# Attention values summed by heads in column halves, with the row factors turned instead of the sums

## The reference, cut to what matters

```
p = masked_softmax(q @ k.T * scale, mask)                       # every branch
o_cmp, o_slc, o_win = p @ v                                      # NSA
o = g[:, :, 0] * o_cmp + g[:, :, 1] * o_slc + g[:, :, 2] * o_win # gates by token and head
y_a = o @ w_branch_nsa[layer]
y_b = dsa_mixer(...) @ w_branch_dsa[layer]
mixed = (gate[..., :D_MODEL] * y_a + gate[..., D_MODEL:] * y_b) @ w_out[layer]
```

## Time and profile before

| what | value |
| --- | --- |
| time, median of 3 runs | 1774.59 us (1774.58 to 1776.01) |
| time of the profiled execution | 1776.0 us |
| its span | 1774.0 us |
| mean granted TensorE clock | 0.979 |
| PE busy | 1672.5 us |
| DVE, ACT, POOL busy | 1250.1, 706.8, 614.2 us |
| attention steps | from 497.7 to about 914 us of the span |

### The profile page before, as it was taken

The page is one execution under the profiler, slowest core; times in us unless marked ns, Lnnn a source line. Parts: engine busy times, 40 slices in busy tenths (PEclk is TensorE's granted clock), DMA queues, the critical chain, the costliest instruction groups (busy, mean ns, idle before and its releaser), DMA issues.

```text
span 1774.0 us, 24401 instructions
## 1 busy us (share of the span) xinstructions
PE 1672.5 (94%) x8648; PEld 1356.2 (76%) x8648; DVE 1250.1 (70%) x2226; ACT 706.8 (40%) x1390; POOL 614.2 (35%) x465
## 2 busy tenths in 40 slices
PE   6789989999999999999998989799999999999997
PEld 5667877888868766778777867688888888887885
DVE  5689788999544656777756605776677676677988
ACT  5543343322155656666642103422222222244445
POOL 3304223322141113343322220644445444444444
PEclk9899999999999999999999999899999999999999
DMA  5102233533151101001005434133223333385443
GB/s 184 48 1 92 71 97 101 168 101 95 54 149 69 76 25 37 25 13 37 25 29 162 146 92 142 42 104 105 89 89 104 123 113 106 133 276 181 146 114 119
DMA packets 153688, 172.13 MB, mean 97 GB/s; under 512 B 19552, under 2 KB 103520, under 8 KB 153312
## 3 DMA queue, kind: packets, MB, share of 16 engines
q1 hardware_dynamic: 153568, 170.57, 30.3%
HBM read 121.00 MB, written 49.55 MB: 96 GB/s over the span
## 4 chain that ended last, share of the span: by engine, by line
PE 73%; DVE 11%; issue 5%; DMA 4%; ACT 3%; POOL 3%; SPq 0%; DVEq 0%; POOLq 0%; ACTq 0%
PE psA L1461 13%; PE psA L1462 13%; PE psA L1463 13%; PE psT L1468 7%; PE psT L1461 5%; PE psT L1463 5%; PE psT L1462 5%; PE psT L1643 5%; PE psA L1527 2%; PE psA L1528 2%; DMA wd<-in_w_down_dram 2%; DVE rotated L1908 1%; DVE equal L1968 1%; POOL w_lo L396 1%; DVE above L1968 1%
## 5 line engine op out<-in xcount | busy, mean ns | idle before, releaser
L396 POOL TENSOR_TENSOR w_lo<-w_raw,w_hi 128x1024 fp32r<-128x1024 f32 (+2 forms) x52 | 119.5, 2306 | 240.3 <-ACT w_hi L391 240.1
L1064 POOL TENSOR_TENSOR w_lo<-w_sum,w_hi 128x1024 fp32r<-128x1024 f32 x44 | 115.6, 2629 | 129.8 <-ACT w_hi L1346 129.8
L1291 ACT ACTIVATE s<-s,nmax 128x640 f32<-128x640 f32 (+7 forms) x192 | 144.3, 752 | 35.6 <-DVE nmax L2081 34.6
L1087 POOL TENSOR_TENSOR w_lo<-act_raw,w_hi 128x512 fp32r<-128x512 f32 x77 | 106.3, 1382 | 107.6 <-ACT w_hi L1375 107.6
L1461 PE MATMUL psA<-w_hi,xTh 128*128 128x512 f32 (+2 forms) x320 | 124.3, 389 | 13.7 <-POOL w_lo L396 9.6
L1468 PE MATMUL psT<-ident,s 128*128 128x128 f32 x816 | 121.9, 278 | 1.5 <-ACT s L1291 0.8
L1462 PE MATMUL psA<-w_lo,xTh 128*128 128x512 f32 (+2 forms) x320 | 120.6, 377 | 0.0
L1463 PE MATMUL psA<-w_hi,xTl 128*128 128x512 f32 (+2 forms) x320 | 120.4, 376 | 0.0
L1468 PEld LDWEIGHTS psT<-ident,s 128*128 128x128 f32 x816 | 91.0, 141 | 26.9 <-issue 16.8
L391 ACT CAST w_hi<-w_raw 128x1024 fp32r<-128x1024 f32 (+2 forms) x52 | 52.4, 1013 | 146.9 <-PE psA L1463 105.9
L2308 DVE TENSOR_TENSOR w_lo<-wd,w_hi 128x512 fp32r<-128x512 f32 x77 | 85.9, 1119 | 24.4 <-ACT w_hi L1382 24.2
(11 more groups left out here) (376 smaller groups left out, 4869.2 us busy)
## 6 DMA issues: line engine op xcount, KB each, us to landing
act_raw<-scratch_act SPq DMA_DIRECT2D x77, 256.0 KB, 3.0
w_raw<-in_w_in_dram SPq DMA_DIRECT2D x28, 512.0 KB, 3.9
scratch_act<-act SPq DMA_DIRECT2D x33, 256.0 KB, 2.2
scratch_act<-act_sum SPq DMA_DIRECT2D x33, 256.0 KB, 2.1
wd<-in_w_down_dram SPq DMA_DIRECT2D x33, 256.0 KB, 3.0
scratch_gates<-gate_out SPq DMA_DIRECT2D x32, 256.0 KB, 3.0
gates<-scratch_gates SPq DMA_DIRECT2D x32, 256.0 KB, 4.1
a<-in_w_gate_dram SPq DMA_DIRECT2D x22, 256.0 KB, 3.2
```

Source lines behind the costliest of these rows:

```text
L396: nc.gpsimd.tensor_tensor(self.lo[n % RING][:, 0:u], self.raw[n % RAW][:, 0:u], self.hi[n % RING][:, 0:u].bitcast(F32), ALU.subtract).then ...
L1064: nc.gpsimd.tensor_tensor(lo2[n % RING][:], block_of(n)[:], hi2[n % RING][:].bitcast(F32), ALU.subtract)\
L1087: nc.gpsimd.tensor_tensor(lo2[slot][:, 0:512], act_raw[n % 6][:], hi2[slot][:, 0:512].bitcast(F32), ALU.subtract)\
L1291: a_.activation(s_sb[v % SR][:, 0:n], s_sb[v % SR][:, 0:n], ACT.Exp, scale=-1.0, bias=nmax[:, BR[a], i, h:h + 1], accum_out=psum_p[:, BR[a ...
```

## The change

What it does, in five parts:

- Values by heads. For each key tile two products with the same weights: the first head of the pair into the lower 64 partitions, the second into the upper 64, each with 128 columns. All key tiles add up in place, there are no two parts, and nothing is filled with zeros. Four heads take 256 columns of the bank instead of 512, and `acc` holds a whole tile of 8 heads.
- Row factors turned. POOL spreads the factors (for slc and win times the gate) over 64 columns for each head (`r_wide`, at `R_LAG` 3), PE turns these 4 blocks once for each tile and branch (key "r", at `O_LAG`), and DVE multiplies the turned factors in PSUM with `acc` in SBUF, once for each tile. The gating of the factors on DVE (L2093) goes.
- No turning back. Everything is added in the layout of the merge: POOL adds `yt` to `ya` once for each slc and win tile. For i >= 4 DSA's product and the last NSA sum are written to `y_raw` directly; for i < 4 ACT rounds `ya` and POOL, instead of DVE, takes the rest.
- Compressed branch. POOL multiplies by its gate ahead of the turning (`c_s`), one more operation of 512 columns a tile; the product has its operands exchanged, and DVE only copies it.
- The chunks of DSA and NSA are split at steps 6 and 7 behind the last unit, where they were at 7 and 9.

```diff
     acc = [sb(work, f"acc{n}", [P, H * HD]) for n in range(2)]
-    yt = [sb(work, f"ytmp{n}", [P, G, 2, HD]) for n in range(2)]
+    yt = sb(work, "ytmp", [P, H * HD])
+    r_wide = sb(work, "row_factors_wide", [P, H, HD])
...
         if group_of(u, O_LAG):
             opened.append(group_of(u, O_LAG))
-            groups6.append(("o", *opened[-1]))
-        if y_of(u):
-            groups6.append(("y", *y_of(u)))
+        if tile_of(u, O_LAG):
+            groups6.append(("r", *tile_of(u, O_LAG)))
...
-    CHUNK_AT = {"dsa": len(units) + O_LAG + 1, "nsa": len(units) + Y_LAG + 1}
+    CHUNK_AT = {"dsa": len(units) + O_LAG, "nsa": len(units) + F_LAG}
...
@@ POOL
-                nc.gpsimd.tensor_tensor(c_p[:], c_p[:], c_st[:, 2, :].unsqueeze(2).to_broadcast([P, H, 64]), ALU.mult)\
+                then(nc.gpsimd.tensor_tensor(c_p[:], c_p[:], c_st[:, 2, :].unsqueeze(2).to_broadcast([P, H, 64]), ALU.mult))
+                nc.gpsimd.tensor_tensor(c_s[:], c_p[:], nsa_gate[:, i, 0:H].unsqueeze(2).to_broadcast([P, H, 64]), ALU.mult)\
                     .then_inc(cp_done, 1)
...
+            if tile_of(u, R_LAG):
+                a, i = tile_of(u, R_LAG)
+                t = t6[a, i]
+                r = psum_r[:, BR[a], i, :].unsqueeze(2).to_broadcast([P, H, HD])
+                pool.wait_ge(rows_done, t + 1)
+                if t:
+                    pool.wait_ge(t_ps, g6["r", *tiles6[t - 1]] + 1)
                 if a == "dsa":
+                    nc.gpsimd.tensor_copy(r_wide[:], r).then_inc(wide_done, 1)
                 else:
+                    nc.gpsimd.tensor_tensor(r_wide[:], r, gate, ALU.mult).then_inc(wide_done, 1)
...
-                    then(nc.gpsimd.tensor_tensor(part[0], part[0], part[1], ALU.add))
-                    nc.gpsimd.tensor_tensor(y, y, part[0], ALU.add).then_inc(y_done, 1)
+                if a == "slc" and i >= HT:
+                    nc.gpsimd.tensor_tensor(y_late("nsa", i), heads(y[:], 4), heads(yt[:], 4), ALU.add).then_inc(y_done, 1)
+                else:
+                    nc.gpsimd.tensor_tensor(y[:], y[:], yt[:], ALU.add).then_inc(y_done, 1)
...
@@ ACT
-                a_.copy(acc[o % 2][:], psT[:, 3, :]).then_inc(acc_out, 1)
+                a_.copy(acc[t % 2][:, 2 * P * g:2 * P * (g + 1)], psT[:, 3, 0:2 * P]).then_inc(acc_out, 1)
...
@@ PE
                 for c in range(k, k + nk):
-                    rows, cols = slice(HD * (c % 2), HD * (c % 2 + 1)), slice(2 * P * (c - k), 2 * P * (c - k + 1))
-                    mm = pe.matmul(bank[rows], val, pT[j % PT][:, cols], start=(c < 2), stop=(c >= n - 2))
-                if n == 1:
-                    mm = pe.matmul(bank[HD:P], zero[:], pT[j % PT][:, 0:2 * P], start=True, stop=True)
+                    for v in range(2):
+                        turned_p = pT[j % PT][:, P * (2 * (c - k) + v):P * (2 * (c - k) + v + 1)]
+                        mm = pe.matmul(bank[HD * v:HD * (v + 1)], val, turned_p, start=(c == 0), stop=(c == n - 1))
...
-            if y_of(u):
-                a, i = y_of(u)
-                pe.wait_ge(y_done, o6[a, i, 1] + 1)
-                y = ya[(ysteps["y", a, i] - 1) % 2]
-                turn4(group(("y", a, i)), [y[:, P * k:P * (k + 1)] for k in range(4)]).then_inc(t_ps, 1)
...
@@ DVE
+                v_.tensor_tensor(yt[:], factors, acc[t % 2][:], ALU.mult).then_inc(t_dve, 1)
```

More of the change, by code:

```diff
@@ L193, in hybrid_block @@
     ya = [sb(work, f"ya{n}", [P, H * HD]) for n in range(2)]
-    acc = [sb(work, f"acc{n}", [P, G * P]) for n in range(2)]
-    yt = [sb(work, f"ytmp{n}", [P, G, 2, HD]) for n in range(2)]
+    acc = [sb(work, f"acc{n}", [P, H * HD]) for n in range(2)]
+    yt = sb(work, "ytmp", [P, H * HD])
+    r_wide = sb(work, "row_factors_wide", [P, H, HD])
     c_st = sb(work, "c_st", [P, 4, H])
@@ L463, in y_of, with tile_of @@
         a, i, h = at(u - Y_LAG)
-        return (a, i) if a in ("slc", "dsa") and h == H - 1 else None
+        return (a, i) if a in ("slc", "dsa") and h == H - 1 and i < HT else None
+    def tile_of(u, lag):
+        a, i, h = at(u - lag)
+        return (a, i) if a and h == H - 1 else None
     def group_of(u, lag):
@@ L504, in by_act, with y_ready, y_free, y_of_tile @@
     def by_act(key):
-        return key[0] in ("ch", "cp") or (key[0] == "y" and key[2] >= HT) or (key[0] == "p" and key[1] % 2 == 0)
+        return key[0] in ("ch", "cp") or (key[0] == "p" and key[1] % 2 == 0)
     act_took = nth([k for k in groups6 if by_act(k)])
     dve_took = nth([k for k in groups6 if not by_act(k)])
-    ysteps = nth([k for k in groups6 if k[0] == "y"])
-    groups_y = list(ysteps)
-    y_halves = {h: nth([k for k in ysteps if (k[2] >= HT) == h]) for h in (False, True)}
+    tiles6 = [k[1:] for k in groups6 if k[0] == "r"]
+    t6 = {k: n for n, k in enumerate(tiles6)}
+    sums6 = {k: n for n, k in enumerate(k for k in tiles6 if k[0] != "dsa")}
+    y_tiles = [("dsa", i) for i in range(HT)] + [("slc", i) for i in range(NT)]
+    def y_ready(eng, a, i):
+        if a == "dsa":
+            eng.wait_ge(t_dve, dve_took["r", a, i])
+        else:
+            eng.wait_ge(y_done, sums6[a, i] + 1)
+    def y_free(eng, a, i):
+        n = y_tiles.index((a, i)) - 2
+        if n >= 2 * HT:
+            eng.wait_ge(y_done, sums6[y_tiles[n]] + 1)
+        elif n >= 0:
+            eng.wait_ge(yl_done, n + 1)
+    def y_of_tile(a, i):
+        return ya[y_tiles.index((a, i)) % 2]
+    def y_late(set_, i):
+        return y_raw[set_][:, :, tok(i - HT)]
     chunks = [(set_, k) for set_ in ("dsa", "nsa") for k in range(KT // 2)]
-    CHUNK_AT = {"dsa": len(units) + O_LAG + 1, "nsa": len(units) + Y_LAG + 1}
+    CHUNK_AT = {"dsa": len(units) + O_LAG, "nsa": len(units) + F_LAG}
     consts = sem("consts")
@@ L1040, in _ @@
                 block_bias(i)
-            if group_of(u, F_LAG):
-                a, i, g = group_of(u, F_LAG)
-                o = o6[a, i, g]
-                n = ysteps["y", "dsa" if a == "dsa" else "slc", i]
-                y = heads(ya[(n - 1) % 2][:, G * HD * g:G * HD * (g + 1)], G)
-                part = [yt[o % 2][:, :, r, :] for r in range(2)]
-                pool.wait_ge(t_dve, dve_took["o", a, i, g])
+            if tile_of(u, R_LAG):
[5 more added lines that the diff above has]
+                    pool.wait_ge(t_ps, g6["r", *tiles6[t - 1]] + 1)
@@ L1232, in chunks_hi @@
             act.wait_ge(pj_done, len(jobs))
-            act.wait_ge(t_act, act_took["y", "dsa" if set_ == "dsa" else "slc", NT - 1])
+            y_ready(act, "dsa" if set_ == "dsa" else "slc", NT - 1)
             for k in range(KT // 2):
-                a_.copy(yTh[set_, 1][:, k, :], y_raw[set_][:, k, :]).then_inc(yc_hi, 1)
+                a_.copy(yTh[set_, 1][:, k, :], y_raw[set_][:, k, :]).then_inc(yh_done, 1)
         for u in range(STEPS6):
@@ L1469, in turn4 @@
             return mm
-        pe.wait_ge(consts, 3)
+        pe.wait_ge(consts, 2)
         def turn_bank(key):
@@ L1594, in m_step @@
             elif m == 0:
-                pe.wait_ge(t_dve, dve_took["y", "slc", HT - 1])
+                pe.wait_ge(yl_done, 2 * HT)
             if m >= 2:
@@ L1636, in _ @@
                 pe.wait_ge(*((t_act, act_took["p", j, 0]) if by_act(("p", j, 0)) else (t_dve, dve_took["p", j, 0])))
-                c0 = 2 * P * (h % G // 2)
-                bank = accumulator(o6[a, i, h // G], k == 0 and c0 == 0)[:, c0:c0 + 2 * P]
+                pair = h % G // 2
+                bank = accumulator(o6[a, i, h // G], k == 0 and pair == 0)[:, P * pair:P * (pair + 1)]
                 for c in range(k, k + nk):
@@ L1682, in _ @@
                 pe.wait_ge(cp_done, i + 1)
-                turn4(group(("cp", i, 0)), [c_p[:, 2 * n:2 * n + 2, :].rearrange("p a w -> p (a w)") for n in range(4)])\
+                turn4(group(("cp", i, 0)), [c_s[:, 2 * n:2 * n + 2, :].rearrange("p a w -> p (a w)") for n in range(4)])\
                     .then_inc(t_ps, 1)
@@ new lines, in scaled @@
+        def scaled(a, i):
+            t = t6[a, i]
+            factors = psT[:, g6["r", a, i] % 3, :]
+            dve.wait_ge(t_ps, g6["r", a, i] + 1)
+            dve.wait_ge(acc_out, o6[a, i, 1] + 1)
+            if a != "dsa":
+                n = sums6[a, i]
+                if n:
+                    dve.wait_ge(y_done, n)
+                v_.tensor_tensor(yt[:], factors, acc[t % 2][:], ALU.mult).then_inc(t_dve, 1)
+            elif i < HT:
+                y_free(dve, a, i)
+                v_.tensor_tensor(y_of_tile(a, i)[:], factors, acc[t % 2][:], ALU.mult).then_inc(t_dve, 1)
+            else:
+                v_.tensor_tensor(y_late("dsa", i), heads(factors, 4), heads(acc[t % 2][:], 4), ALU.mult).then_inc(t_dve, 1)
```

121 lines of the change are left out of this document (54 added, 67 removed).

## The result

The changed kernel took 1741.66 us, median of 4 runs (1739.05 to 1742.68), against 1774.59 us of the kernel before in the same session (4 runs, 1771.54 to 1776.01). The ratio is 0.9814, with a 95% interval of 0.9801 to 0.9826: 33 us or 1.9% faster. The profiled execution took 1741.32, its span 1739.6 us.

The account below looks back on a forecast made before the run. PE, busy 94% of the span, was taken to bound the kernel. Terms -17.6 - 10.9 - 5.0 + 2.0 + 4.8 - 3.4 - 1.2 = -31.3 took 1776.0 to 1744.7, less 1.4 for the median: 1743.5 us, range 1729 to 1762.

Parts of the forecast that it names:

- Turnings: PE in attention: 160 fewer turning records of acc and ya at 0.11 us each, -17.6 us.
- Values: PE's value products: 816 starts of 0.11 us replace 464 of 0.217, 89.8 instead of 100.7 us, -10.9 us.
- The bounds above (+41, +87 beside it): Value starts: +41 us if a 51 ns load adds to each, +87 if a start has a floor regardless of columns.
- What isn't realised: Two short-tile stretches: ACT's and DVE's latencies hold back half of the 9.7 us PE saves there, +4.8 us.
- PE's waits: Waits before turning acc (6.9 us) and ya (3.0) lose their cause; half counted, -5.0 us, bounds 0 and -9.9.
- POOL's order: POOL works in order; spread factors stand behind window additions, gating in the compressed chain: +2 us, bounds 0 and 8.
- a sign of being wrong: PE's waits for the spread factors or the compressed chain coming to more than 5 us.
- The start of the merge: After the last values: chunks begin about 3 us later instead of 8; 5 us less 1.6 counted elsewhere, -3.4 us.
- the clock, -1.2: Behind the wait before merge step 4: low clock costs 2.4 us; a shorter wait may avoid it, half counted.
- the smaller products are not cheaper: Rival at the 816 value starts: the values term turns from -10.9 to +31, 1785 us; chance 0.09.
- The turn-round of DVE and ACT: Rival: PE's relief kept only from 697 us on and at the merge, 5 us of new waits, 1757 us; chance 0.16.
- All waits go: Rival: -9.9 us of waits, short tiles in full, clock keeps its level; -44 us, 1730; chance 0.09.

Follow-up runs that it names:

- turned_thrice: Changed kernel with each group of four factor turnings made three times into the same bank, 192 turnings more; 1759.60 us, ratio 0.9908.
- values_256: Changed kernel with the value products put back to one of 256 columns for each key tile, the halves' addition left out; 1744.24 us, ratio 0.9822.
- best_values_256: Changed kernel with spread factors and gates issued earlier, compressed turning and product later, and value products of 256 columns put back; 1738.59 us, ratio 0.9792.
- halves_apart: Changed kernel with, for each head pair, all value products of the lower 64 partitions first, then all upper ones; 1790.99 us, ratio 1.0085.
- after_again: The changed kernel run once more, nothing altered; 1741.09 us, ratio 0.9804 to the kernel before.
- spread_first: Changed kernel with POOL's spread factors ahead of the window additions, which go to steps 10, 18, 26 and 29; 1734.01 us, ratio 0.9767.
- nsa_sum_late: Changed kernel with the last addition of the NSA sum made five times on POOL, starting the chain into the merge later; 1745.05 us, ratio 0.9827.
- before_values_128: Kernel before with only the value products changed, to two of 128 columns for each key tile; stale second halves still processed; 1770.34 us, ratio 0.9970.

## Why the prediction was right, and where it was not

The forecast was 1743.5 us, and 1741.7 came. That it is so near is in part luck. The stage was 3.3 to 4.7 us shorter than its terms, and the parts that the change does not touch, ahead of the attention and behind merge step 5, were 2.6 us longer in the profile. By its steps:

- **Turnings, -17.6.** Measured 15.4 to 16.6 (turned_thrice). The price of 0.11 stands in the rows; about a tenth of it is hidden.
- **Values, -10.9.** Measured 7.4 to 8.8 (values_256) and 9.1 (best_values_256). Run by run it is as worked out: 1.31 us for 5 tiles (1.51 with 256 columns), 1.75 for 7 (0.19 less than before), 1.97 for 8. The bounds above (+41, +87 beside it) did not come: records with loads of 64 columns and 128 columns of their own stand 0.11 us apart. The rule of the Trainium skill that I set against this step (TensorE: Matmul & The Clock Gate, The mechanism: a load overlaps running matmuls only where the row groups differ) is not borne out by the trace. In halves_apart 16 records in a row use all rows and the same column half, each with a load of its own, and the 32 starts stand (3.33 - 0.27) / 31 = 0.10 us apart. The reason that I gave, that a load of 51 ns fits under 109, is not what the rows show. I took the 51 from the excess of the first record and not from PEld's own records. In this run of 32:

```profile
L1689 PEld LDWEIGHTS psT<-pT,v_slc x32: 133/137/137, 935.3 to 938.3; 128*64 128x64 f32 x32
```

A load's record lasts 0.137 us (in the kernel before 0.133 to 0.137 as well), longer than the 0.10 from one start to the next, so loads overlap matmuls and each other. The overhead of some 60 cycles for each matmul that the Trainium skill names (TensorEngine Tiling (Array Packing), Instruction Overhead) adds nothing here: starts of 256 columns stand 0.217 us apart, and starts of 128 columns 0.11, half as much.

- **What isn't realised, +4.8.** The two terms above were -28.5 together, -23.7 with this one; measured are 22.8 to 25.7. The step held.
- **PE's waits, -5.0, and POOL's order, +2.** Both were mis-sized, and they cancel. The waits for `acc` and `ya` went entirely, -9.9. The new waits are 5.6 for the spread factors and 1.4 for the gated compressed factors, +7.0 in the changed kernel and 5.8 in after_again. Net -2.9 to -4.1, where I had -3.0; that the sum of the two came out is luck. The prediction named more than 5 us of these waits as a sign of being wrong, and this is the step that failed, though the sum came out right: it named the place (behind the window additions, steps 10 to 28) but priced only the gatings. What it should have priced is the queue: POOL's rows above have 5.2 us for four additions, while 32 steps of the first tiles take 38.7 us, 1.2 each, so a spread behind four additions is late by steps (3.1 us at most). spread_first shows the cause: with the order changed, all waits for the spread factors are gone.
- **The stage as a whole.** The terms that fall into it gave -25.1 (1.6 of the sum lie behind the last value). Measured are -29.8 and -28.4. With 156 of the turnings in the stage, at 0.104 or 0.096 us, and 0.7 of the old waits behind it, the measured terms give -16.2 - 8.8 - 9.2 + 7.0 = -27.2 against the changed kernel's profile and -15.0 - 7.4 - 9.2 + 5.8 = -25.8 against after_again's. The 2.6 us beyond, in both, are not attributed to anything by a run. The clock is not the reason: over the stage it was granted 0.99 before, 0.98 in the changed kernel and 0.97 in after_again, so it can only have worked against the gain. The prediction had no term for that, and no run prices it.
- **The start of the merge, -3.4, with 1.6 counted before, and the clock, -1.2.** Together -6.2; measured -7.2 and -5.6. Of the 1.6, the 0.9 for two turnings was one group too many: eight turnings stood behind the last value before, and the four of the factors stand there now. The wait of about 2.5 us before merge step 4 is there, 2.6. That the clock may or may not fall behind it is what two executions of one kernel show: 5.6 us for step 4 in one, 7.2 in the other, and 8.1 before the change. nsa_sum_late shows that the chain sets this place.

Of the rivals, that the smaller products are not cheaper is refuted by values_256, best_values_256 and before_values_128. The turn-round of DVE and ACT does not bind: what PE saves comes through for about nine tenths of the turnings. "All waits go" would have needed spread_first's order; with it and the gates ahead the kernel stands at 1730.5, which was this rival's number, though made in another way.

## What to carry to other kernels

Where products leave half of the columns of the array idle, put the two that shall run side by side next to each other: here the order of the two innermost loops was worth 49 us. Check it before anything else. When work moves to an engine that works in order, look at the longest burst ahead of it in the queue and not at its own duration; here 0.6 us of work was 3 us late, and moving it ahead of the burst was worth 3.9 to 5.3 us, half of what the values' part had brought. And when a wait is left at the end of a chain, read what the DMA queue did before the transfer that ends it: the gates could have gone out 10 us earlier. To price a part of the change, compare the stretch it lives in and the granted clock of that stretch, not the whole time alone.

## What was not expected of the hardware

- Records of one column half in a row, with a weight load each, start 0.10 to 0.11 us apart, no dearer than turnings, while each load's own record lasts 0.137 us.
- With equal work and a wait of 2.6 to 2.7 us, the granted clock fell to 0.50 in one execution of the changed kernel and stayed at 1.00 in another. With the wait gone, merge step 4 took 5.5 us, the time of the full clock, in all five profiles.
- On POOL a spread by copy of 128 x 512 takes 0.61 us, the same with a multiplication 1.05, an addition of two tiles 1.28, and 1.70 from start to start if each waits for the one before.
- The same program differs by 2 us in the part ahead of the attention from one execution to the next. Over all profiles this part spans 4 us, with the granted clock at 0.96 where it is long and at 0.98 where it is short, and the part behind merge step 5 spans 7.
